# Six projection chunks of a hybrid decoder layer: the two x terms of the high weights in one wide product, the halves of the bank added by VectorE

## The reference, cut to what matters

```
xn = rms_norm(h, ln1_w)
proj = xn @ w_in          # [256, 1024] @ [1024, 9744]
a_qkv, gq, gk, gv, gog, glr, merge = split(proj)
```

## Time and profile before

| what | value |
|---|---|
| median of 3 runs | 1251.53 us (1251.39 to 1255.16) |
| span of the profiled execution, first to last instruction | 1248.5 us |
| instructions | 17019 |
| PE busy | 1169.1 us (94%) |
| DVE busy | 445.6 us (36%) |
| ACT busy | 250.3 us (20%) |
| chain that ended last | PE 59%, DMA 35%, DVE 2% |
| DMA | 456.98 MB, mean 366 GB/s |

### The profile page before, as it was taken

The page is one execution under the profiler, slowest core; times in us unless marked ns, Lnnn a source line. Parts: engine busy times, 40 slices in busy tenths (PEclk is TensorE's granted clock), DMA queues, the critical chain, the costliest instruction groups (busy, mean ns, idle before and its releaser), DMA issues.

```text
span 1248.5 us, 17019 instructions
## 1 busy us (share of the span) xinstructions
PE 1169.1 (94%) x7215; PEld 604.2 (48%) x7216; DVE 445.6 (36%) x766; ACT 250.3 (20%) x353; POOL 15.9 (1%) x30
## 2 busy tenths in 40 slices
PE   9999999999999999899899989898989989899997
PEld 9998988888633343333333333333333333333332
DVE  5754546666532233222222222222322222222232
ACT  4544445544401010001000000000000001000012
POOL 2200000000000000000000000000000000000000
PEclk9999999999999999999999999999999999999999
DMA  9645333377999999999999999999999999999996
GB/s 296 219 169 186 135 135 135 135 277 282 371 417 425 431 431 427 430 430 429 431 433 427 431 430 429 430 430 434 433 428 431 433 427 431 435 427 432 421 428 278
DMA packets 50031, 456.98 MB, mean 366 GB/s; under 512 B 5988, under 2 KB 6136, under 8 KB 31400
## 3 DMA queue, kind: packets, MB, share of 16 engines
q1 hardware_dynamic: 49544, 455.09, 87.7%
q10 hardware_dynamic: 448, 1.32, 0.3%
HBM read 455.35 MB, written 1.05 MB: 366 GB/s over the span
## 4 chain that ended last, share of the span: by engine, by line
PE 59%; DMA 35%; DVE 2%; SPq 2%; ACT 1%; issue 1%; DVEq 0%
PE ps L1384 57%; DMA ring<-in_w_up_dram 22%; DMA arena<-in_w_up_dram 12%; PE ps L1891 1%; DMA ring<-in_w_in_dram 1%; ACT w_split L588 0%; SPq L397 0%; DVE w_split L892 0%; SPq L399 0%; PE ps L1777 0%; PE ps L1573 0%; SPq L414 0%; DVE arena L1062 0%; SPq L391 0%; PE ps L1680 0%
## 5 line engine op out<-in xcount | busy, mean ns | idle before, releaser
L1384 PE MATMUL ps<-ring,arena 128*64 128x512 f32 x2304 | 523.2, 608 | 50.9 <-DMA ring<-in_w_up_dram 50.9
L1384 PEld LDWEIGHTS ps<-ring,arena 128*64 128x64 f32 x2304 | 163.9, 140 | 378.8 <-issue 300.3
L1384 PE MATMUL ps<-arena 128*64 128x512 f32 (+3 forms) x920 | 202.7, 563 | 17.0 <-DMA arena<-in_w_up_dram 16.1
L1296 DVE TENSOR_SCALAR arena<-ps 128x512 f32<-128x512 f32 x32 | 22.1, 692 | 487.3 <-PE ps L1384 487.3
L892 DVE TENSOR_TENSOR w_split<-ring,w_split 128x2048 fp32r<-128x2048 f32 x48 | 109.8, 2291 | 108.4 <-ACT w_split L588 108.1
L1384 PEld LDWEIGHTS ps<-arena 128*64 128x64 f32 (+1 forms) x920 | 78.2, 149 | 128.4 <-issue 100.2
L796 ACT ACTIVATE arena<-arena 128x512 f32<-128x512 f32 x32 | 20.2, 631 | 552.6 <-DVE arena L1296 552.6
L1384 PE MATMUL ps<-w_split,x_split 128*128 128x512 f32 x528 | 123.5, 392 | 0.7 <-ACT arena L624 0.5
L1384 PEld LDWEIGHTS ps<-w_split,x_split 128*128 128x128 f32 x528 | 98.4, 188 | 21.8 <-issue 1.2
L588 ACT ACTIVATE w_split<-ring 128x2048 fp32r<-128x2048 f32 x47 | 89.6, 1911 | 70.7 <-PE ps L1384 62.5
L1384 PE MATMUL ps<-x_split,w_split 128*128 128x256 f32 x768 | 94.7, 284 | 0.1
(11 more groups left out here) (251 smaller groups left out, 624.8 us busy)
## 6 DMA issues: line engine op xcount, KB each, us to landing
ring<-in_w_up_dram SPq DMA_DIRECT2D x40, 4096.0 KB, 31.1
ring<-in_w_down_dram SPq DMA_DIRECT2D x46, 2048.0 KB, 30.2
arena<-in_w_up_dram SPq DMA_DIRECT2D x14, 4096.0 KB, 31.1
ring<-in_w_in_dram SPq DMA_DIRECT2D x17, 2048.0 KB, 7.8
arena<-in_w_down_dram SPq DMA_DIRECT2D x14, 2048.0 KB, 30.0
ring<-in_w_up_dram SPq DMA_DIRECT2D x12, 2048.0 KB, 23.1
arena<-in_w_up_dram SPq DMA_DIRECT2D x4, 2048.0 KB, 23.5
ring<-in_w_up_dram SPq DMA_DIRECT2D x8, 1024.0 KB, 8.7
```

The lines of the kernel that those rows point to most:

```text
L1296: dve.tensor_scalar(glu_c, ps[bank][:, :], LIMIT, None, ALU.min).then_inc(glu_ok, 1)
L1384: return pe.matmul(dst, lhsT, rhs, start=start, stop=stop, skip_group_check=True)
```

## The change

In chunks 3, 4, 6, 7, 9 and 10 each half m of a unit has a bank of its own, `ps[m]`. For each of the 8 tiles the high weights are multiplied with x's high and low halves at once, in one matmul of 512 columns whose results land in the two halves of the bank; the low weights times the high x, 256 columns, are added to the first half. So a half unit has 8 matmuls of 512 and 8 of 256 columns. VectorE adds the two halves of the bank on the way out, by a `tensor_reduce` over pairs of elements that lie 256 apart: `halves_added(u)`, two instructions a unit, at the head of VectorE's iteration u. ScalarE has no part in these units' evacuation. As every unit now uses both banks, half m of a unit waits for the evacuation of half m of the unit just before (`bank_free`). Counts of semaphores that other steps wait on are recomputed by `act_outs` and `dve_outs`. The semaphore `warmed`, which nobody waited on, is dropped.

```
+        def by_weights(u):
+            return u // 2 < QKV_CHUNKS + 2 and u // 2 not in BY_ROWS
...
-                act.wait_ge(proj_done, u + 1)
-                bank = ps[u % 2]
...
-                act.activation(dst, src, ACT.Copy).then_inc(proj_out, 1)
...
+            def halves_added(u):
+                c, s = u // 2, u % 2
+                for m in range(2):
+                    if m == 0:
+                        dve.wait_ge(tile_done, halves_done(u))
+                    else:
+                        dve.wait_ge(proj_done, u + 1)
...
+                    dve.tensor_reduce(dst, ps[m].rearrange("p (i t) -> p t i", i=2), AX_X, ALU.add).then_inc(added, 1)
             for u in range(UNITS):
+                if by_weights(u):
+                    halves_added(u)
...
+            def bank_free(u, b):
+                if by_weights(u - 1):
+                    pe.wait_ge(added, dve_outs(u) - 1 + b)
+                else:
+                    pe.wait_ge(proj_out, act_outs(u) - 1 + b)
...
-                if u >= 2:
-                    pe.wait_ge(proj_out, u - 1)
                 for m in range(2):
-                    dst = ps[u % 2][:, m * SEQ:m * SEQ + SEQ]
+                    bank_free(u, m)
                     for k in range(KT):
-                        ins = product(dst, [split_w(u, i)[:, k, m * P:m * P + P] for i in range(2)],
-                                      [x_split[:, i, k, :] for i in range(2)], k == 0, k == KT - 1)
-                ins.then_inc(proj_done, 1)
+                        w = [split_w(u, i)[:, k, m * P:m * P + P] for i in range(2)]
+                        mm(ps[m].rearrange("p (i t) -> p i t", i=2), w[0], x_split[:, :, k, :], k == 0, False)
+                        ins = mm(ps[m][:, 0:SEQ], w[1], x_split[:, 0, k, :], False, k == KT - 1)
+                    ins.then_inc((tile_done, proj_done)[m], 1)
```

More of the change, by code:

```diff
@@ L246, in layer @@
         proj_done, proj_out, tile_done = sem("proj_done"), sem("proj_out"), sem("tile_done")
+        added = sem("added")
         oa_high_ok, oa_low_ok, ob_low_ok, mixed_low_ok = (
@@ L263, in layer @@
         res_ok = [sem(f"res_ok{t}") for t in range(TT)]
-        wo_half, part_ok, sel0_ok, xin_half_ps, xin_half_ok, warmed = (
-            sem(n) for n in ("wo_half", "part_ok", "sel0_ok", "xin_half_ps", "xin_half_ok", "warmed"))
+        wo_half, part_ok, sel0_ok, xin_half_ps, xin_half_ok = (
+            sem(n) for n in ("wo_half", "part_ok", "sel0_ok", "xin_half_ps", "xin_half_ok"))
         lg_ps, lg_shift, lg_exp, taken_ok, count_ps, turns_ok = (
@@ L316, in split_w, with act_outs, dve_outs, halves_done @@
             return w_split[:, u % SPLITS, part, :].rearrange("p (k n) -> p k n", k=tiles)
+        def by_weights(u):
+            return u // 2 < QKV_CHUNKS + 2 and u // 2 not in BY_ROWS
+        def act_outs(u):
+            return sum(1 for v in range(u) if not by_weights(v))
+        def dve_outs(u):
+            return sum(2 for v in range(u) if by_weights(v))
+        def halves_done(u):
+            return dve_outs(u) // 2 + 1 + sum(1 for c in BY_ROWS if c < u // 2)
         def tiles_done(c):
-            return BY_ROWS.index(c) + 1
+            return BY_ROWS.index(c) + 1 + dve_outs(2 * c) // 2
         O_BANK = ((5, 2), (6, 7))
@@ L570, in _ @@
             act.wait_ge(early_ok, 2)
-            act.activation(warm[:, 0:1], epsc[:, 0:1], ACT.Sqrt).then_inc(warmed, 1)
+            act.activation(warm[:, 0:1], epsc[:, 0:1], ACT.Sqrt)
             act.wait_ge(x_in[1], 16)
@@ L724, in _ @@
                 if u == S_GLA:
-                    act.wait_ge(proj_out, 2 * C_MERGE)
+                    act.wait_ge(proj_out, act_outs(2 * C_MERGE))
                     act.activation(g_o[:, :, :], gog[:, :, :], ACT.Sigmoid).then_inc(sig_ok, 1)
@@ L774, in _ @@
             act.activation(gate[:, :, :], gate[:, :, :], ACT.Exp).then_inc(lg_exp, 1)
-            act.activation(warm[:, 1:2], epsc[:, 0:1], ACT.Sigmoid).then_inc(warmed, 1)
+            act.activation(warm[:, 1:2], epsc[:, 0:1], ACT.Sigmoid)
             for t in range(TT):
@@ L1084, in gate_products @@
                        .then_inc(gl_ops, 1)
+            def halves_added(u):
[5 more added lines that the diff above has]
+                        dve.wait_ge(proj_done, u + 1)
+                    if c < QKV_CHUNKS:
+                        dst = qkT[:, c % 3, c // 3, 2 * s + m, :]
+                    else:
+                        if u == 2 * C_GQ and m == 0:
+                            dve.wait_ge(pick_ok, 1)
+                        dst = (gqT if c == C_GQ else gkT)[:, s * 512 + m * SEQ:s * 512 + m * SEQ + SEQ]
+                    dve.tensor_reduce(dst, ps[m].rearrange("p (i t) -> p t i", i=2), AX_X, ALU.add).then_inc(added, 1)
             for u in range(UNITS):
+                if by_weights(u):
+                    halves_added(u)
                 if U_PB <= u < U_WO and (u - U_PB) % 2:
@@ L1117, in _ @@
                     dve.wait_ge(vecT_ok, 1)
-                    dve.wait_ge(proj_out, 2 * C_GV)
+                    dve.wait_ge(added, dve_outs(2 * C_GV))
                     gate_logits()
@@ L1181, in _ @@
                 if U_PA <= u < U_PB:
-                    dve.wait_ge(proj_out, PROJ_UNITS)
+                    dve.wait_ge(proj_out, act_outs(PROJ_UNITS))
                     for t in range(TT):
@@ L1484, in projection @@
                     for t in range(TT):
-                        if first and u + t >= 2:
-                            pe.wait_ge(proj_out, u + t - 1)
+                        if first:
+                            bank_free(u, t)
                         for k in range(4):
@@ L1510, in branch_a @@
                 else:
-                    pe.wait_ge(proj_out, PROJ_UNITS)
+                    pe.wait_ge(proj_out, act_outs(PROJ_UNITS))
                 for t in range(TT):
@@ L1556, in at_scores @@
                 if h == 0:
-                    pe.wait_ge(proj_out, 2 * QKV_CHUNKS)
+                    pe.wait_ge(proj_out, act_outs(2 * QKV_CHUNKS))
+                    pe.wait_ge(added, dve_outs(2 * QKV_CHUNKS))
                 for g in range(NG):
@@ L1658, in _ @@
                     pe.wait_ge(at_o, NH)
-                    pe.wait_ge(proj_out, 2 * C_GOG)
+                    pe.wait_ge(proj_out, act_outs(2 * C_GOG))
                     gla_update()
```

1 line of the change is left out of this document (added).

## The result

The changed kernel takes 1259.2 us in the median of 6 runs (1256.65 to 1260.69), the kernel before 1251.89 us in as many (1250.6 to 1255.16). The ratio is 1.0056, with a 95% interval of 1.0041 to 1.0072: slower by about 7.0 us, 5.1 to 9.0. The profiled execution took 1257.98 us, with a span of 1256.2 us, 7.7 more than before; its distance of 1.8 us from time to span is that of all timed runs of this kernel (1.7 to 2.0).

What follows compares the result with a forecast made beforehand. TensorE bounds the dense stage, and delays there reach the end one to one. Waits 9.8, clock 1.7, probabilities 0.2, less gain 2.45: +9.3 us on span 1248.5, plus 3.0 to the median, gives 1260.8 us; range 1256.0 to 1263.0.

Steps and rivals of the forecast that it cites:

- The direction and the mechanism: Slower, chance 0.86: TensorE waits for banks whose reductions stand late in VectorE's queue behind low splits and prepare steps.
- The price of a reduction: Each of VectorE's 24 new reductions of 512 PSUM elements: between 0.68 and 1.20 us, 1.20 taken.
- the upper bound: VectorE's reduction at doubled cost per element, as in ScalarE's reads of every fourth fp32: 1.20 us.
- rival 1: VectorE's reductions run at the contiguous rate, 0.68 us each: time 1256.2 to 1259.6, middle 1257.9 us; chance 0.41.
- the walk: Following VectorE's queue unit by unit: TensorE idles before units 7, 9, 10, 13, 15, 20 and 22, 9.8 us in sum.
- The product's gain: TensorE's units in the changed chunks take 5.56 instead of 5.76 us: 0.20 us a unit, 2.45 us in all.
- one of the prediction's own signs of being wrong: In the changed chunks, a wide product followed by a narrow one costs other than the sum of 227 and 120 ns.
- The clock: One loss of 1.7 us after the 4.1 us wait before unit 7; a second possible after 2.5 us before unit 10.
- One to one to the end: Every microsecond the dense stage gets longer delays the experts' full-rate stream and the kernel's end by the same amount.
- Rival 2: The later experts' stage swallows the dense stage's delay: not slower, 1251.5 us; chance 0.07.
- rival 3: In the changed chunks the bank is never late and only the gain is left: 1249.1 us; chance 0.05.
- The 3.0 us that it added from span to median: Whole kernel: the timed median before, 1251.5 us, lay 3.0 above the profiled span, 1248.5; this difference was left unchanged.

Runs made afterwards that it cites:

- experiment 1: Changed kernel with two more PSUM banks for odd units in chunks 3, 4, 6 and 7, VectorE's queue unchanged; 1249.9 us, ratio 0.9996 against the kernel before.
- experiment 5: Changed kernel with its two banks, but VectorE's prepare steps 5 to 9 moved to iterations 9, 10, 15 and 16; 1250.49 us, ratio 0.9998.
- Experiment 7: Changed kernel with every tensor_reduce issued twice, about 1.4 us a half; 1262.18 us, ratio 1.0089 against the kernel before.
- experiment 6: The four-bank kernel of experiment 1 with each half's eight wide products first, then its eight narrow ones; 1249.2 us, ratio 0.9987.
- experiment 2: The four-bank kernel of experiment 1 with the high and low x of each tile laid side by side; 1249.9 us, ratio 0.9986.
- experiment 3: Changed kernel with 28 products of ones into an unused bank after unit 6, in TensorE's first wait; 1258.24 us, ratio 1.0056.
- the repeat: The changed kernel, unedited, measured once more for the spread of its runs; 1258.89 us, ratio 1.0069 against the kernel before.

## Why the prediction came out as it did

**The direction and the mechanism** were right: the profile has the waits for the bank ahead of units 7, 9 and 10, behind the low split and a `prepare` step; experiments 1 and 5 take the loss away from either side.

**The price of a reduction** is the step that failed: 1.20 us was taken, 0.69 was measured. The doubling came from ScalarE's read of every fourth element in SBUF; VectorE reading PSUM in pairs 1 KB apart pays nothing for the step. The Trainium skill's line rule ("SBUF — State Buffer", Specifications), 8 bytes in PSUM, gives no size for the penalty; read as a doubling, as the prediction read it, it puts the price at the upper bound. This trace disagrees for VectorE's reads (686 ns), and the measurement decides. So rival 1 has the right price, and its three long waits are nearly those of the profile: 3.6, 0.7 and 2.5 forecast, 3.5, 0.7 and 2.2 measured. Its 0.2 and all that the walk put in the attention did not come. The forecast's 4.1 + 1.2 + 2.5 + 0.7 + 0.2 + 0.6 + 0.5 = 9.8 is 6.3. Experiment 7, with 1.4 us a half, shows that the walk finds the places once the price is high enough, six of seven, and that it puts too much in the attention. Rival 1's 1257.9 us lies 1.3 under the measured median, the forecast's 1260.8 lies 1.6 over it: the time does not choose between them, the trace does.

**The product's gain** was mis-sized the other way: 2.45 us forecast, 1.3 measured. A unit takes 16 x 353 ns = 5.65 us, not 5.56, against 5.76 before: 0.11 us a unit. A pair that costs other than the sum of the two gaps was one of the prediction's own signs of being wrong, and it came. The two gaps do not simply add when widths alternate; grouping gives back 4 ns a pair (experiment 6), and the jump in x is no part of it (experiment 2). The Trainium skill's rule on the gap ("TensorE: Matmul & The Clock Gate", Back-to-back issue gap), which the page gives for the gap of a matmul by itself, would have given 0.5 us; the measured gain lies between it and the forecast.

**The clock.** One loss of 1.7 us was counted, and 1.73 is what experiment 3 measures for it. The second, named with its wait of 2.5 us but not counted, is there in one profile of the changed kernel, after 2.10 us, and not in the other, after 1.99. The length alone does not decide: in the experts' stage of the kernel before, waits of 2.04 to 2.13 us (nine of them, the prediction counted eight) cost nothing.

**One to one to the end** held nearly: the last dense stage's windows are unchanged at 8 us later, the experts' DMA piece is 7.92 us later, the end 7.7. Rival 2 (the later stage swallows the delay) and rival 3 (the bank is never late) are out.

**The sum.** In the profiled execution: waits 6.3, clock 1.7, probabilities 0.2, less 1.3 of gain: 6.9, and the late load of chunk 2 gives up to 1.0 more, against 7.7 to 7.9 seen. The median moved by 7.0 us by the ratio, 8.6 in the repeat (1.0069). The forecast of 9.3 was 3.5 too high in the waits and took off 1.2 too much for the gain, and these two errors lean against each other; the repeat, whose profile has the second loss of clock, comes nearer still. The 3.0 us that it added from span to median came out too, by luck: a run lies 1.7 to 2.0 us above its own span, and the rest is that the profiled execution lay under the median both times. The closeness of the forecast owes as much to all this as to the steps.

## What to carry to other kernels

When an evacuation moves to another engine, write down that engine's queue at the moment the bank is wanted, not its busy share: VectorE was 36% busy, and small steps of up to 3.3 us that could as well run later, ahead of reductions of 0.7 us, made the kernel 7 us slower. Look at the same time at how many units of slack the banks give; two more banks, or the movable steps put where no bank is waited for, each took the loss away here (ratios 0.9996 and 0.9998). A gain of 0.1 us in each of twelve units does not pay for a single wait of TensorE of 2 us, which may cost the clock on top of itself.

## What the runs showed of the hardware

A `tensor_reduce` on VectorE that reads PSUM in pairs 1 KB apart takes 686 ns for 512 elements, as a copy of neighbours does (680). Matmuls of 512 and 256 columns in turn take 353 ns a pair, grouped by width 349, and 347 would be the sum of the two gaps. A wait of 3.32 us (three profiles) or 4.05 us (one) in a full stream of products was each time followed by a lower clock, for a loss of 1.6 to 1.7 us; waits of 1.90 and 1.99 us were not, one of 2.10 and one of 2.34 us were. With 28 products of ones in the place of the first 1.74 us of that wait, the 1.74 us left over cost no clock.

The experts' stage has many more such waits, for weights. Over the twelve kept profiles, 32 products took 8.4 us or more instead of 7.09 behind 126 of 130 waits of 2.5 us or more, behind 26 of 29 between 2.2 and 2.5 us, behind 9 of 132 between 1.9 and 2.2 us (all nine of 2.14 us or more), and behind none of the 120 shorter ones.
